# Local attention with both key blocks merged into one 128-column score tile

## The reference, cut to what matters

```python
def sliding_window_sink_attention(q, k, v, sinks, valid):
    ...
    kb, vb = band(k), band(v)           # block before and own block: 256 keys
    scores = einsum('bnqhgd,bnkhd->bnhgqk', qb, kb) * scale
    diff = (BLOCK + arange(BLOCK))[:, None] - arange(2 * BLOCK)[None, :]
    mask = ((diff >= 0) & (diff < WINDOW))[None] & kvalid[:, None, :]
    scores = where(mask[None, :, None, None], scores, -inf)
    ...
    probs = softmax(concatenate([scores, sink], axis=-1), axis=-1)[..., :-1]
    o = einsum('bnhgqk,bnkhd->bnqhgd', probs, vb)
```

## Time and profile before

| | |
|---|---|
| median of 3 runs | 974.29 us (974.1 to 974.49) |
| profiled execution, its own time | 973.93 us |
| its span, first to last instruction | 972.1 us |
| busy: PE, DVE, ACT, POOL | 98%, 66%, 51%, 27% |
| mean granted TensorE clock | 0.998 of 2.4 GHz |

### The profile page before, as it was taken

How to read it: one execution, slowest core, us unless ns; L and a number is a source line. 1 busy time by engine, 2 the same in 40 slices (tenths; PEclk the granted TensorE clock), 3 DMA queues, 4 the chain that set the end, 5 groups by cost and what they waited for, 6 DMA issues and landing times.

```text
span 972.1 us, 13078 instructions
## 1 busy us (share of the span) xinstructions
PE 956.1 (98%) x4854; PEld 805.9 (83%) x4854; DVE 641.6 (66%) x951; ACT 493.0 (51%) x911; POOL 259.1 (27%) x205
## 2 busy tenths in 40 slices
PE   7999999999999999999999999999999999999997
PEld 6988888888888888888888888888888887888886
DVE  5677777937787687846656798699557985312314
ACT  5445665724435655625447777423557982221212
POOL 2216200003226200002352010340325885224131
PEclk9999999999999999999999999999999999999999
DMA  9332201133422301133323011132320113233312
GB/s 299 101 122 69 88 23 44 50 124 91 142 87 87 104 27 44 44 130 83 109 91 96 31 44 44 44 96 83 117 74 1 44 44 94 80 93 102 129 44 87
DMA packets 64991, 80.39 MB, mean 83 GB/s; under 512 B 5520, under 2 KB 48656, under 8 KB 64928
## 3 DMA queue, kind: packets, MB, share of 16 engines
q1 hardware_dynamic: 63024, 76.64, 24.8%
q10 hardware_dynamic: 1904, 2.88, 0.9%
HBM read 77.42 MB, written 2.10 MB: 82 GB/s over the span
## 4 chain that ended last, share of the span: by engine, by line
PE 53%; issue 30%; DVE 6%; ACT 5%; POOL 3%; DMA 1%; POOLq 0%; ACTq 0%; DVEq 0%
PE ps L1956 14%; PE ps L1958 14%; PE ps L1957 14%; PE ps L2013 1%; PE ps L2015 1%; PE ps L2014 1%; PE ps L2477 1%; PE ps L2492 1%; DVE wlo L1609 1%; DVE sp L1703 1%; ACT spr L967 1%; POOL small L562 1%; POOL small L575 1%; DMA x<-in_x 1%; PE ps L2505 1%
## 5 line engine op out<-in xcount | busy, mean ns | idle before, releaser
L607 POOL TENSOR_TENSOR wlo<-raw,whi 128x2048 fp32r<-128x2048 f32 (+1 forms) x22 | 97.0, 4410 | 183.6 <-ACT whi L961 174.2
L1956 PE MATMUL ps<-whi,hhi 128*128 128x512 f32 (+1 forms) x320 | 115.7, 362 | 1.0 <-ACT sp L1059 0.3
L1958 PE MATMUL ps<-whi,hlo 128*128 128x512 f32 (+1 forms) x320 | 114.5, 358 | 0.0
L1957 PE MATMUL ps<-wlo,hhi 128*128 128x512 f32 (+1 forms) x320 | 114.5, 358 | 0.0
L1956 PE MATMUL ps<-hhi,whi 128*128 128x512 f32 x288 | 113.4, 394 | 0.0
L1958 PE MATMUL ps<-hhi,wlo 128*128 128x512 f32 x288 | 112.3, 390 | 0.0
L1957 PE MATMUL ps<-hlo,whi 128*128 128x512 f32 x288 | 112.2, 390 | 0.0
L961 ACT ACTIVATE whi<-raw 128x2048 fp32r<-128x2048 f32 (+1 forms) x29 | 53.0, 1826 | 82.5 <-PE ps L1958 74.1
L1280 DVE TENSOR_TENSOR wlo<-raw,whi 128x2048 fp32r<-128x2048 f32 (+1 forms) x29 | 63.6, 2193 | 37.5 <-ACT whi L728 30.9
L728 ACT ACTIVATE whi<-raw 128x2048 fp32r<-128x2048 f32 (+1 forms) x29 | 52.1, 1796 | 69.4 <-PE ps L1958 69.4
L2013 PE MATMUL ps<-hhi,whi 128*128 128x512 f32 x192 | 76.8, 400 | 0.0
(11 more groups left out here) (329 smaller groups left out, 2323.2 us busy)
## 6 DMA issues: line engine op xcount, KB each, us to landing
raw<-in_w_in SPq DMA_DIRECT2D x42, 1024.0 KB, 5.3
raw<-in_w_out SPq DMA_DIRECT2D x12, 1024.0 KB, 5.0
raw<-in_w_in SPq DMA_DIRECT2D x10, 512.0 KB, 3.9
raw<-in_w_branch_swa SPq DMA_DIRECT2D x4, 1024.0 KB, 5.0
raw<-in_w_branch_sb SPq DMA_DIRECT2D x4, 512.0 KB, 3.5
x<-in_x ACTq DMA_DIRECT2D x3, 512.0 KB, 6.8
out<-x SPq DMA_DIRECT2D x3, 512.0 KB, 2.6
ws<-in_spatial_w SPq DMA_DIRECT2D x2, 512.0 KB, 6.9
```

Source lines behind the costliest of these rows:

```text
L607: pool.tensor_tensor(wlo[s][:, 0:n, :], raw[s][:, 0:n, :], whi[s][:, 0:n, :].bitcast(F32), ALU.subtract).then_inc(slab_split, 1)
L1956: pe.matmul(out_ap, lhsT=lhi(k), rhs=rhi(k), start=first and k == 0, stop=False, skip_group_check=True)
L1957: pe.matmul(out_ap, lhsT=lhi(k), rhs=rlo(k), start=False, stop=False, skip_group_check=True)
L1958: m = pe.matmul(out_ap, lhsT=llo(k), rhs=rhi(k), start=False, stop=last and k == n - 1, skip_group_check=True)
```

## The change

Both key blocks are merged in the score tile: the own scores are copied over those of the block before where the own key is seen (key column at or below the query), by `copy_predicated` with a triangular constant as the predicate. No masks are added; in block 0 a matmul writes the large negative fill into the 112 padding columns. The sink is written as column 128, so the maximum and the exponential of 129 columns take it in. One set of 128 weights for a query then serves both blocks, and is transposed once. The output is values of the block before times all weights, plus the step of values (`vd`: own values less those of the block before) times the own weights, which are the transposed weights multiplied by the 0/1 tile `own_keys`: the high part on VectorE, the low part on GpSimd (`window_own_low`). The steps of values are made ahead of the loop by GpSimd (`v_step`), and split by ScalarE and VectorE (`value_steps_low`). Windows come in another order (`turn_of`): first all blocks of heads 0 to 7, then of heads 8 to 15. The final gain's load moves from before slab 2 to before slab 28, and its place in memory holds `vd`.

```diff
+def turn_of(w):
+
+    return w % 8 // 2, 2 * (w // 8) + w % 2
...
-            late(row_gain[:], rows_to_all(a["final_norm_gain_2"], 0, D))
             for j in range(2, len(SLABS2)):
+                if j == 28:
+                    sp.wait_ge(swo_done, 16)
+                    sp.dma_start(row_gain[:], rows_to_all(a["final_norm_gain_2"], 0, D)).then_inc(final_loaded, 16)
                 slab2(j)
...
+            pool.memset(v_meta[0:96, :], 0.0).then_inc(vw_clear, 1)
...
                 split2_lo(j)
+                if j == 10:
+                    pool.wait_ge(tokw_copied, 3)
+                    pool.wait_ge(vw_clear, 2)
+                    pool.tensor_tensor(v_step[:, 1:, :], tokw[:, 1:, 1152:1280], tokw[:, 0:3, 1152:1280], ALU.subtract)\
+                        .then_inc(v_step_ready, 1)
+                    pool.tensor_tensor(v_step[:, 0, :], tokw[:, 0, 1152:1280], v_meta[:], ALU.subtract)\
+                        .then_inc(v_step_ready, 1)
...
+            def window_own_low(w):
+
+                pool.wait_ge(tw_lo, 10 + w + 1)
+                pool.tensor_tensor(by_head(pwt[:, 1, 1, :]), by_head(pwt[:, 1, 0, :].bitcast(F32)),
+                                   insert_dim(own_keys.bitcast(F32), 1, 4), ALU.mult).then_inc(window_own_lo, 1)
+
             for w in range(16):
 
-                nk = P + (META if w < 4 else P)
+                p4 = four_heads(pw, w)[:, :, 0:P]
+                at_ = 128 + 4 * (w % 2)
                 pool.wait_ge(inv_ready, w + 1)
-                for i in (2 * w, 2 * w + 1):
-                    at_ = 128 + 4 * (i % 4)
-                    pool.tensor_tensor(pw[:, i % 4, :, 0:nk], pw[:, i % 4, :, 0:nk],
-                                       insert_dim(small2[:, at_:at_ + 2], 2, nk), ALU.mult).then_inc(pw_ready, 1)
+                pool.tensor_tensor(p4, p4, insert_dim(small2[:, at_:at_ + 4], 2, P), ALU.mult).then_inc(pw_ready, 1)
+                if w:
+                    window_own_low(w - 1)
                 if w >= 2:
                     window_gated(w - 2)
...
+                if half == 0:
+                    act.wait_ge(v_step_ready, 2)
+                    copy(vd[:, :, :, 0:64], v_step[:].rearrange("p t (g d) -> p t g d", g=2), 0.5).then_inc(vw_hi, 1)
...
             def transposed_hi(w):
-                for kb in range(2):
-                    act.wait_ge(tw_done, 10 + 2 * w + kb + 1)
-                    if w and kb == 0:
-                        act.wait_ge(swo_done, w)
-                    copy(pwt[:, 0, kb, :], ps[:, 4 + kb, :]).then_inc(tw_hi, 1)
+                act.wait_ge(tw_done, 10 + w + 1)
+                if w:
+                    act.wait_ge(swo_done, w)
+                copy(pwt[:, 0, 0, :], ps[:, 4 + w % 2, :]).then_inc(tw_hi, 1)
...
+                for c in range(4):
+                    m = 4 * (w % 2) + c
+                    last = act.activation(four_heads(pw, w)[:, c, 0:P + 1], four_scores(w)[:, c, 0:P + 1], ACT.Exp,
+                                          bias=small2[:, 32 + m:33 + m], accum_out=small2[:, 64 + m:65 + m])
...
-                    dve.tensor_tensor(tokm[:, 0, :], ps[64:64 + META, 2, 0:256], tokm[:, 0, :], ALU.add)\
+                    dve.tensor_tensor(tokm[:, 0, 0:P], ps[64:64 + META, 2, 0:P], tokm[:, 0, 0:P], ALU.add)
+                    link(dve.tensor_tensor(v_meta[96:P, :], ps[96:P, 2, P:2 * P], v_meta[96:P, :], ALU.add))
+                    dve.tensor_scalar(v_meta[96:P, :], v_meta[96:P, :], rows_of_four[96:P, 3:4], None, ALU.mult)\
                         .then_inc(tokw_copied, 1)
...
+            def value_steps_low():
+
+                dve.wait_ge(vw_hi, 2)
+                for g in range(2):
+                    last = low(vd[:, :, g, 64:128], v_step[:, :, 64 * g:64 * g + 64], vd[:, :, g, 0:64], 0.5)
+                last.then_inc(vw_lo, 1)
...
+                    if (half, t) == (0, 1):
+                        value_steps_low()
+
+            dve.sem_inc(rope2_done, 5)
...
             def transposed_lo(w):
 
-                for kb in range(2):
-                    dve.wait_ge(tw_hi, 10 + 2 * w + kb + 1)
-                    low(pwt[:, 1, kb, :], ps[:, 4 + kb, :], pwt[:, 0, kb, :]).then_inc(tw_lo, 1)
+                dve.wait_ge(tw_hi, 10 + w + 1)
+                low(pwt[:, 1, 0, :], ps[:, 4 + w % 2, :], pwt[:, 0, 0, :]).then_inc(tw_lo, 1)
+                dve.tensor_tensor(by_head(pwt[:, 0, 1, :]), by_head(pwt[:, 0, 0, :].bitcast(F32)),
+                                  insert_dim(own_keys.bitcast(F32), 1, 4), ALU.mult).then_inc(window_own_hi, 1)
...
             def window_max(w):
...
+                u, m, z = turn_of(w)[1], 4 * (w % 2), four_scores(w)
+                dve.wait_ge(sw_scored, 2 * w + 2)
+                link(dve.copy_predicated(z[:, :, 0:P], insert_dim(own_to_query, 1, 4), z[:, :, P:]))
+                link(dve.tensor_copy(z[:, :, P:P + 1], insert_dim(sink[:, 4 * u:4 * u + 4], 2, 1)))
+                dve.reduce_max(small2[:, 32 + m:36 + m], z[:, :, 0:P + 1], AX.X, negate=True).then_inc(bias_ready, 1)
...
             def window_norm(w):
...
+                m = 4 * (w % 2)
                 dve.wait_ge(sw_exp, 2 * w + 2)
+                dve.reciprocal(small2[:, 128 + m:132 + m], small2[:, 64 + m:68 + m]).then_inc(inv_ready, 1)
...
+                    b = ps[:, i % 4, :].rearrange("p (e k) -> p e k", e=2)
+                    if n == 0:
+                        pe.matmul(b[:, :, 0:frm], lhsT=ident_r, rhs=insert_dim(mask_pad, 1, 2), start=True, stop=True,
+                                  skip_group_check=True)
                     for e in range(2):
-                        q = qw[:, 2 * (i % 8) + e, P * n:P * n + P]
+                        q = qw[:, 4 * u + 2 * (i % 2) + e, P * n:P * n + P]
                         for part in range(2):
-                            m = pe.matmul(b[:, e, :], lhsT=q, rhs=kw[:, part, u // 2, at_key:at_key + nk],
-                                          start=False, stop=part == 1, skip_group_check=True)
+                            m = pe.matmul(b[:, e, frm:], lhsT=q, rhs=kw[:, part, u // 2, at_key:at_key + nk],
+                                          start=part == 0, stop=part == 1, skip_group_check=True)
...
+                for c in range(4):
+                    m = pe.matmul(ps[:, 4 + w % 2, P * c:P * c + P], lhsT=four_heads(pw, w)[:, c, 0:P], rhs=ident[:],
+                                  is_transpose=True)
+                m.then_inc(tw_done, 1)
...
+                before, change = vw[:, n - 1, g, :] if n else vwm[:, g, :], vd[:, n, g, :]
                 for part in range(2):
                     pe.matmul(o, lhsT=before, rhs=pwt[:, part, 0, :], start=part == 0, stop=False)
-                for part in range(2):
-                    m = pe.matmul(o, lhsT=own, rhs=pwt[:, part, 1, :], start=False, stop=part == 1)
-                m.then_inc(swo_done, 1)
+                pe.wait_ge(window_own_hi, w + 1)
+                pe.matmul(o, lhsT=change, rhs=pwt[:, 0, 1, :], start=False, stop=False)
+                pe.wait_ge(window_own_lo, w + 1)
+                pe.matmul(o, lhsT=change, rhs=pwt[:, 1, 1, :], start=False, stop=True).then_inc(swo_done, 1)
...
-                            pe.wait_ge(ysw_ready, {0: 14, 4: 15, 6: 16}[k])
+                            pe.wait_ge(ysw_ready, {0: 8, 4: 15, 6: 16}[k])
```

More of the change, by code:

```diff
@@ L222, in build @@
         gate_sw = sb("gate_sw", [P, 8, SEQ])
-        tokm = sb("tokm", [META, 3, 256])
+        r_tokm = region(3 * KB)
+        tokm = sb("tokm", [META, 1, 256], F32, r_tokm)
+        v_step = sb("v_step", [P, NT, P], F32, r_tokm + KB)
         yw = sb("yw", [P, 2, 2, P], F32, r_sbias)
@@ L974, in _ @@
             transposed_x(DEPTH, 0, 3)
-            act.wait_ge(late_loaded, 112)
+            act.wait_ge(late_loaded, 96)
             split2(2)
@@ L1087, in _ @@
             unit(29)
-            copy(tokm[:, 0, :], ps[0:META, 2, 0:256]).then_inc(tokm_copied, 1)
+            copy(tokm[:, 0, 0:P], ps[0:META, 2, 0:P])
+            copy(v_meta[96:P, :], ps[32:64, 2, P:2 * P]).then_inc(tokm_copied, 1)
             act.wait_ge(meta_z, 1)
@@ L1093, in _ @@
             act.wait_ge(tokw_copied, 3)
[L1094 to L1095 removed]
+            act.wait_ge(vw_clear, 2)
+            copy(vwm[96:P, :, 0:64], v_meta[96:P, :].rearrange("p (g d) -> p g d", g=2), 0.5)
             copy(vw[:, :, :, 0:64], tokw[:, :, 1152:1280].rearrange("p t (g d) -> p t g d", g=2), 0.5)\
@@ L1614, in _ @@
             transposed_x(DEPTH, 0, 3)
-            dve.wait_ge(late_loaded, 112)
+            dve.wait_ge(late_loaded, 96)
             rows8 = consts_f[:, CONSTS - 8:]
@@ L1788, in _ @@
                 d = slice(1152 + 64 * g, 1216 + 64 * g)
-                low(vwm[0:META, g, 64:128], tokm[:, 0, 128 + 64 * g:192 + 64 * g], vwm[0:META, g, 0:64], 0.5)
-                last = low(vw[:, :, g, 64:128], tokw[:, :, d], vw[:, :, g, 0:64], 0.5)
-            last.then_inc(vw_lo, 1)
```

(27 more changed lines are left out.)

68 lines of the change are left out of this document (28 added, 40 removed).

## The result

The changed kernel takes 978.66 us (median of 6 runs, 977.59 to 979.2) against 974.21 for the kernel before (6 runs): a ratio of 1.0044, interval 1.0031 to 1.0057. It is slower by 4.45 us; 980.8 was predicted. The profiled execution took 977.73 us, span 975.9, 3.80 over that of before. The kernel before took 974.21 beside the changed kernel, and 974.11, 974.13 and 973.77 beside the later experiments.

What follows compares the result with a forecast made beforehand. TensorE, busy 98% of the span, was taken to bound the kernel before; 973.93 + 4.3 (loop) - 0.6 (its start) + 2.9 (ahead) = 980.5 for the profiled execution, 980.8 as median, range 968 to 985.

Steps and rivals of the forecast that it cites:

- the chain through own_low: Window loop: VectorE's own_hi, GpSimd's own_low, then TensorE's fourth value product; next turn at T + 4.92, taken as 5.0 us.
- The port: Window loop: VectorE's own_hi and GpSimd's own_low, both on SBUF tensors, don't overlap; own_low runs T + 3.08 to T + 4.36.
- Part turns: Six window turns where GpSimd also does part_low (another 1.28 us): GpSimd's sum 5.01 plus 0.69 held by own_hi, 5.7 each.
- The last turn: Last window turn: VectorE's 2.29 us slab subtraction stays in the way, 0.75 more, so 5.75 us.
- The sum of the loop: 15 window turns: 8 x 5.0 + 6 x 5.7 + 5.75 = 79.95 us against 75.69, +4.3.
- Ahead of the loop: Before slab 13: added VectorE and GpSimd work of 3.4 us less 0.62 cover, +2.8 of TensorE waiting, 0.1 at next gate.
- the loop's start: Before w = 1: smaller first GpSimd product, four fewer transposes, window 3's scores without masks; counted as -0.6 us.
- the two bounds: VectorE's 128x512 copy_predicated in PSUM: at least 0.64 to 0.69 us, at most two passes, 1.3; 0.69 taken.
- rival C: Window loop: own_low shuts out copy_predicated too, window_out late by 0.4 each turn, +6, 987 us; chance 0.1.
- Rival B: Window loop: own_low costs 1.04, 3.4 us less, with partial losses ahead of the loop: 974 to 977; chance 0.18.
- Rival A: Window loop: TensorE or GpSimd sets the turn, own_hi and own_low don't block each other; -7.2, 969.4 us; chance 0.27.
- the prediction's second loop: Window loop: window_out also waits for GpSimd's out_lo of two windows before, behind own_low and gating; 5.00 us a turn.

Runs made afterwards that it cites:

- the moves: Changed kernel with v_step before slab 10 and value_steps_low before the last gate: 976.3 us; with value_steps_low alone moved: 977.53 us.

## Why the prediction was right, and where its sizes were off

*TensorE stops setting the turn; the chain through own_low does.* Right: 6.5 us of waits for own_low, 13 times, the chain of the turns through own_low, and work added to TensorE hidden. The kernel without the products shows what was there to gain (14.5 us against the changed kernel, 10.0 against the kernel before).

*The port.* Right as a mechanism, and shown: one operand moved to PSUM gives 5.2 us back, 6.0 in the loop. Mis-sized: I let own_low start only at the end of own_hi, then run its full 1.28, so 0.6 of waiting. Its loss is 0.38 to 0.40. The prediction's own rows had the difference: behind VectorE's end at 803.94 GpSimd took 0.61 more for a product of 0.73. The turn is 4.82 instead of 5.0, eight of them 38.3 instead of 40.0.

*Part turns.* Right that GpSimd's sum sets them; its terms were 1.00, 1.26, 0.69, 0.70 and, without the conflict, 1.24, to which I added the whole 0.69 of own_hi where 0.43 was lost: 5.32 instead of 5.7, six of them 31.9 instead of 34.2.

*The last turn.* 6.85 instead of 5.75. The prediction added 0.75 for VectorE's slab 21. But the subtraction (2.29 alone) is held up by own_low, which started at 802.83 and took 1.67, and the gating of 0.74 then by the subtraction, until 806.63. Window_out waited for the low output behind the gating:

```profile
803.50 3.13 DVE L1649 TENSOR_TENSOR wlo<-raw,whi 128x2048 fp32r<-128x2048 f32 x1 [0.16 <-ACT whi L1002]
808.04 0.86 DVE L1910 TENSOR_TENSOR yw<-ps,other_part 64x256 f32<-64x256 f32 x2 [1.40 <-POOL qw L691]
```

```profile
804.45 2.79 POOL L683 TENSOR_TENSOR yw<-yw,gate_sw 128x256 f32<-128x256 f32 x1
807.20 0.74 POOL L691 TENSOR_TENSOR qw<-yw,qw 128x256 fp32r<-128x256 f32 x1
```

*The sum of the loop:* +1.4 instead of +4.3, made of -1.7 for turns without a part, -2.3 for those with one and +1.1 for the last. This is the term that makes 980.8 too high; that the sum isn't further off is in part luck, as the last turn's error goes the other way.

*Ahead of the loop.* Predicted +2.9 and, for the loop's start, -0.6, so +2.3; T of the first turn lies 2.42 later than before (734.80 against 732.38). TensorE is 2.57 late at slab 13, 2.83 at the first scores (718.81 against 715.98), and gains 0.4 back by the first T, as GpSimd's first weights start 3.02 later than before (727.68 against 724.66) and TensorE waits 1.3 us for them instead of 0.4. The part of value_steps_low was right (0.7); the moves show 0.9 for v_step with what it shifts, and 0.7 for the position against slab 12, where the prediction had 1.46 and 1.0. Together 1.4 + 2.4 = 3.8, the difference of the two profiled executions.

*copy_predicated* costs 0.69, the lower of the two bounds, and isn't shut out by GpSimd, so rival C is gone. Rival B fails by own_low's price, 1.29. Rival A was to decide if less than 0.5 of a turn is lost to the port; 0.4 is lost, and it doesn't. It had only the loop through own_low and the value products, 4.2. With the conflict gone a turn still takes 4.44, through window_out, own_low, gating and low output, which is the prediction's second loop less the 0.69 that it gave to own_hi (4.3). The load of the final gain and the looser wait show no wait of TensorE.

## What to carry to other kernels

When work is taken from the engine that sets the time, write out the loops through the other engines with the buffer that closes each: here a two-buffer output tile tied VectorE's next output to GpSimd's last operation, and the new product went into that loop. A VectorE operation with two SBUF inputs and a GpSimd operation on SBUF tensors hardly overlapped here, so count the later one behind the earlier one; where one of VectorE's operands also lies in PSUM, reading it from there removed the conflict at the same duration (0.68). And when an engine is full ahead of a join, new work in its queue there costs its whole length (0.7 for value_steps_low), which went away when the same work stood where the engine was idle.

## What the runs showed of the hardware

The shut-out is not quite whole. In the changed kernel own_low is issued at 746.84 and own_hi ends at 746.68 + 0.68 = 747.36, which leaves 0.52 to wait; it took 1.67 where it takes 1.29 without the conflict, so 0.38 was lost and 0.14 was not. The Trainium skill (SBUF — State Buffer, Who interferes with whom) calls the shared ports an exclusive lock and says, of VectorE's two-port modes, that the one that issues later is fully blocked; the measurement is 0.38 of 0.52. What is not lost hardly depends on how long the wait is. In a part turn own_hi was the later one:

```profile
751.10 1.06 POOL L714 TENSOR_TENSOR pw<-pw,small 128x512 f32<-128x512 f32 x1
```

```profile
751.50 1.21 DVE L1899 TENSOR_TENSOR pwt<-pwt,consts_r 128x512 fp32r<-128x512 f32 x1
```

It had 0.66 to wait and lost 0.53. The slab subtraction at 803.50 had 1.00 to wait and lost 0.84, the gating at 804.45 had 2.18 and lost 2.05. So 0.13 to 0.16 us of each operation is not lost, on either engine. A reason was not tested.

The clock granted to TensorE fell to 0.50 of 2.4 GHz for 3.4 us in two traces, from 671.2 and from 671.7, just behind a wait of TensorE of 2.5 us; starts of its 512-column products then stand 0.43 apart instead of 0.23. In the trace of the changed kernel the same wait stands without a fall.

A copy_predicated of 128x512 float32 within PSUM, with the predicate in SBUF, took 0.68 to 0.70 in all 16 turns, as long as a product of the same size.
